# A two-block sequence model on one core: the opening and FFN edits together with another form of retention's read-out

## What is computed

```
first_block:   n = rms_norm(x); proj = n @ w_in
               ya = s5_branch(proj[:512])          # two-way state-space scan, 32 groups, GLU
               yb = sgu_branch(...)                # spatial gating
               h += (gate_a*(ya @ w_proj_a) + gate_b*(yb @ w_proj_b)) @ w_out
               h += memory_cross_attention(...)
               h += (silu(hn @ w_gate) * (hn @ w_up)) @ w_down
second_block, twice (l = 0, 1):
               z = rmsnorm(x) @ w_in[l]            # queries, keys, values of four mixers, gates
               yA = forgetting_attention   yB = dsa_attention
               r  = retention(rope(qC), rope(kC)/8, vC)       # 8 heads of 64
               yC = head_groupnorm(r) * silu(gC)   yD = sliding_window_gqa
               x += sum_n(sigmoid(gate_n) * (y_n @ w_branch_n)) @ w_out[l]
               x += (silu(a) * b) @ w_down[l]      # a, b = causal_dwconv(h @ w_up)
out = rmsnorm(x)

retention, as the kernel takes it, for head h and token n:
    r[n] = sum_{m <= n} (q[n] . k[m]) * g_h^(n-m) * v[m]
```

## Time and profile before

| | us |
|---|---|
| median of three executions | 3000.81 (3000.4 to 3000.95) |
| the profiled execution, its own time | 3000.99 |
| span of its trace | 2999.2 |
| PE busy | 2965.2 (99%) |
| DVE, ACT, POOL busy | 1559.7, 1345.9, 1308.2 |
| mean granted TensorE clock | 0.998 |

### The profile page before, as it was taken

One profiled execution on the slowest core, in us unless ns is written; L12 is line 12 of the kernel. 1 busy time (PEld: TensorE's weight loads), 2 busy tenths in 40 slices (PEclk: granted clock), 3 DMA queues, 4 the chain that ended last, 5 costly groups with the idle time before them and its releaser, 6 DMA issues.

```text
span 2999.2 us, 41533 instructions
## 1 busy us (share of the span) xinstructions
PE 2965.2 (99%) x15950; PEld 2461.9 (82%) x15950; DVE 1559.7 (52%) x2363; ACT 1345.9 (45%) x2274; POOL 1308.2 (44%) x930
## 2 busy tenths in 40 slices
PE   8999999999999999999999999999999999999998
PEld 7778887789988878888888888888788888888887
DVE  7875351497824978672116433177877521273312
ACT  5443344455533446564234443244565532354432
POOL 5335574410154543134454554554332354554443
PEclk9999999999999999999999999999999999999999
DMA  5234333233233522123333333244231233333322
GB/s 160 81 114 141 95 124 99 74 113 109 82 101 84 149 73 86 50 71 99 96 98 95 95 98 97 84 114 137 72 88 45 72 95 99 95 95 95 99 98 71
DMA packets 215043, 288.25 MB, mean 96 GB/s; under 512 B 42698, under 2 KB 122626, under 8 KB 213186
## 3 DMA queue, kind: packets, MB, share of 16 engines
q1 hardware_dynamic: 212354, 280.41, 31.4%
q0 software_dynamic: 880, 2.99, 0.3%
q10 hardware_dynamic: 1616, 2.23, 0.2%
HBM read 270.33 MB, written 4.72 MB: 92 GB/s over the span
## 4 chain that ended last, share of the span: by engine, by line
PE 92%; DVE 4%; ACT 2%; POOL 1%; issue 1%; DMA 0%; ACTq 0%; SPq 0%; DVEq 0%
PE half L871 75%; PE half L1201 2%; PE half L1204 2%; PE half L1203 2%; PE half L1354 2%; PE half L1340 2%; POOL wL L3402 1%; PE half L1411 1%; PE half L1318 1%; PE half L1323 1%; DVE arena L2388 1%; PE half L1126 0%; PE half L1143 0%; DVE rms L2379 0%; PE half L1397 0%
## 5 line engine op out<-in xcount | busy, mean ns | idle before, releaser
L3402 POOL TENSOR_TENSOR wL<-slot,wH 128x512 fp32r<-128x512 f32 (+1 forms) x904 | 1276.5, 1420 | 1661.5 <-ACT wH L1521 1660.5
L1521 ACT ACTIVATE wH<-slot 128x512 fp32r<-128x512 f32 (+1 forms) x904 | 558.2, 624 | 1074.3 <-PE half L871 1068.5
L871 PE MATMUL half<-nH,wH 128*128 128x512 f32 x2048 | 809.3, 395 | 4.5 <-ACT arena L1534 2.3
L871 PE MATMUL half<-nH,wL 128*128 128x512 f32 x2048 | 798.1, 390 | 0.0
L871 PE MATMUL half<-nL,wH 128*128 128x512 f32 x2048 | 797.7, 389 | 0.0
L871 PE MATMUL half<-arena_split,wH 128*128 128x512 f32 (+1 forms) x2432 | 736.0, 385 | 1.0 <-POOL wL L3402 0.6
L871 PEld LDWEIGHTS half<-arena_split,wH 128*128 128x128 f32 x2432 | 451.1, 188 | 94.0 <-POOL wL L3402 2.8
L871 PE MATMUL half<-arena_split,wL 128*128 128x512 f32 (+1 forms) x1216 | 466.4, 384 | 0.0
L871 PEld LDWEIGHTS half<-nH,wH 128*128 128x128 f32 x2048 | 384.4, 188 | 99.7 <-issue 19.3
L871 PEld LDWEIGHTS half<-nH,wL 128*128 128x128 f32 x2048 | 384.5, 188 | 81.9
L871 PEld LDWEIGHTS half<-nL,wH 128*128 128x128 f32 x2048 | 384.7, 188 | 78.2 <-issue 1.4
(11 more groups left out here) (404 smaller groups left out, 3656.2 us busy)
## 6 DMA issues: line engine op xcount, KB each, us to landing
slot<-in_w_in SPq DMA_DIRECT2D x344, 256.0 KB, 2.7
slot<-in_w_up SPq DMA_DIRECT2D x400, 128.0 KB, 2.2
slot<-in_w_down SPq DMA_DIRECT2D x132, 256.0 KB, 2.7
slot<-in_w_branch SPq DMA_DIRECT2D x64, 256.0 KB, 2.7
slot<-in_w_out SPq DMA_DIRECT2D x48, 256.0 KB, 2.8
arena<-arena SPq DMA_DIRECT2D x40, 256.0 KB, 4.4
slot<-in_w_gate SPq DMA_DIRECT2D x48, 128.0 KB, 2.3
arena<-in_w_gate SPq DMA_DIRECT2D x40, 128.0 KB, 2.3
```

The lines of the kernel that those rows point to most:

```text
L871: mm = pe.matmul(dst, lhsT, rhs, start=(k == 0 and m == 0), stop=(k == last and m == 2))
L1521: act.activation(wH[:, p, 0:cols], slot[:, s, 0:cols], ACT.Copy).then_inc(weights_high, 1)
L3402: pool.tensor_tensor(wL[:, p, 0:cols], slot[:, s, 0:cols], plainly(wH[:, p, 0:cols]), ALU.subtract)\
```

## The change

It has three parts. **Opening:** `plain` of the second half goes behind unit 3 of `zv0` instead of unit 1, `turn_u` and `turn_v` one or two units later, `taps(0)` one. ACT rounds the first units of `zv0` in other places, one of them ahead of its first big copy. The copies into `bd` go from POOL to ACT. SP stores `x_kept` four loads later. DVE makes `gather_taps(0)` amid `inputs_matrix(1)`. **FFN:** ACT keeps "U2" at g = 2 before it waits for S4; DVE multiplies the first two groups out earlier, one in front of P7's rest and one in front of P3's, and makes the rests of P4 and of the next P1 and P5 earlier. **Retention:** values are stationary (128 rows by 64 columns, the two heads on the two halves of the array's columns) and probabilities move (512, 384, 256 and 128 columns), which leaves channels on partitions; ACT copies that into `kC`, PE transposes it (`ret_back`), ACT copies again into `otm`. SiLU of gC goes behind the last copy.

```
-S5_STEPS = [("plain", 1, 1), ("turn_u", 0, 2), ("turn_v", 0, 3), ("taps", 0, 6), ("drive", 0, 8), ("turn_v", 1, 10),
+S5_STEPS = [("plain", 1, 3), ("turn_u", 0, 4), ("turn_v", 0, 5), ("taps", 0, 7), ("drive", 0, 8), ("turn_v", 1, 10),
...
+RETAINED = [("out", 0), ("back", 0), ("out", 1), ("back", 1), ("out", 2), ("out", 3), ("back", 2), ("back", 3)]
...
-                if n == 6:
+                if n == 10:
                     read_out(sp, "ahx0")
...
+                def retained_read(what, i):
+                    pe.wait_ge(S["heads_out_read"], PRIMED + l * ALL_OUTS + OUTS["ret"] + RETAINED.index((what, i)) + 1)
...
-                    else:
-                        pe.wait_ge(S["heads_out_read"], PRIMED + l * ALL_OUTS + OUTS["ret"] + max(i - 1, 1))
+                    elif i >= 2:
+                        retained_read("back", i - 2)
+                    for j in range(NB):
+                        for p in range(2):
+                            mm = pe.matmul(ps[i % 2][HD * p:HD * p + HD, O_AT + j * P:O_AT + T],
+                                           vC[:, j, (2 * i + p) * HD:(2 * i + p) * HD + HD],
+                                           ret_probs[:, i % 2, p, ret_at[j]:ret_at[j] + T - j * P],
+                                           start=(j == 0), stop=(j == NB - 1), skip_group_check=True)
+                    mm.then_inc(S["ret_out"], 1)
+
+                def ret_back(i):
+                    retained_read("out", i)
                     for b in range(NB):
...
+                        mm = pe.transpose(ps[i % 2][:, O_AT + b * P:O_AT + b * P + P], ret_turned[:, i, b * P:b * P + P], ident)
                     mm.then_inc(S["ret_out"], 1)
...
-                for i in range(1, PAIRS):
-                    ret_scores(i)
-                    ret_out(i - 1)
-                ret_out(PAIRS - 1)
+                ret_scores(1)
+                ret_out(0)
+                ret_scores(2)
+                ret_back(0)
+                ret_out(1)
+                ret_scores(3)
+                ret_back(1)
+                ret_out(2)
+                ret_out(3)
+                ret_back(2)
+                ret_back(3)
...
+            round_units("azv0", 0, 0, [0], 512)
             plain_x(0)
-            round_units("azv0", 0, 0, [0], 512)
+            round_units("azv0", 0, 0, [1], 512)
...
                     token_sum_high("ass_ff", 3)
+                    keep(name, "U2", "P6")
                 summed_until(act, "a", g, "S4")
                 product_high(name, "P3")
-                keep(name, "U2", "P6")
+                if g > FIRST_PRODUCTS:
+                    keep(name, "U2", "P6")
...
-            inputs_matrix(1)
-            gather_taps(0)
+            inputs_matrix(1, lambda: gather_taps(0))
```

More of the change, by code:

```diff
@@ L211 @@
 TURNS = turns_before(len(STEPS))
[L212 to L213 removed]
+OUTS = {"fox": 0, "dsa": PAIRS, "ret": 2 * PAIRS, "swa": 4 * PAIRS}
+ALL_OUTS = 5 * PAIRS
+RETAINED = [("out", 0), ("back", 0), ("out", 1), ("back", 1), ("out", 2), ("out", 3), ("back", 2), ("back", 3)]
 class Weave:
@@ L1435, in _ @@
                 pe.wait_ge(S["roped"], PRIMED + l * 6 + 6)
-                pe.wait_ge(S["heads_out_read"], PRIMED + l * ALL_OUTS + OUTS["ret"] + 3)
+                retained_read("back", 2)
                 for it in WEAVE_S.its:
@@ L1678, in _ @@
             angles_whole(0)
+            round_units("azv0", 0, 0, [2], 512)
             circle(0)
-            round_units("azv0", 0, 0, range(1, SPLITS), 512)
+            round_units("azv0", 0, 0, [3], 512)
             act.wait_ge(S["s5_bbar"], 4)
@@ L1714, in _ @@
                     plain_x(q)
+                    act.wait_ge(S["s5_zeros_set"], 2)
+                    for n in range(2):
+                        for g in range(2):
+                            at = slice(STATE * g, STATE * g + STATE)
+                            act.activation(bd[at, n, :, CHAN * g:CHAN * g + CHAN], b_bar[n][at, :, :], ACT.Copy)\
+                               .then_inc(S["s5_zeros_set"], 1)
                 elif task == "turn_u":
@@ L2228, in _ @@
                         decays(1)
[L2230 to L2233, removed]
+                for what, i in RETAINED:
+                    act.wait_ge(S["ret_out"], l * len(RETAINED) + RETAINED.index((what, i)) + 1)
+                    act.activation((ret_turned if what == "out" else otm)[:, i, :], ps[i % 2][:, O_AT:O_AT + T], ACT.Copy)\
+                       .then_inc(S["heads_out_read"], 1)
+                    if what == "out" and i + 2 < PAIRS:
                         decays(i + 2)
-                    if i == 0:
+                    if (what, i) == ("out", 0):
                         stack_high("key", "swa")
+                    if (what, i) == ("back", 0):
                         stack_high("swa", 0)
-                    if i == 1:
-                        read_out(act, "bgC", l)
-                        act.activation(gC, gC, ACT.Silu).then_inc(S["gc_ready"], 1)
+                read_out(act, "bgC", l)
+                act.activation(gC, gC, ACT.Silu).then_inc(S["gc_ready"], 1)
                 gates_used = []
@@ L2596, in split_rows, with inputs_matrix @@
                 return v.rearrange("p e (s c) -> p e s c", s=count)
-            def inputs_matrix(q):
+            def inputs_matrix(q, amid=None):
                 if q:
@@ L2607, in inputs_matrix @@
                 first = mark(dve.tensor_tensor(t[0], l_im, b_im, ALU.mult))
+                if amid:
+                    amid()
                 dve.tensor_tensor(v[1], l_re, b_im, ALU.mult)
@@ L3012, in _ @@
                     dve.sem_inc(drained[h], 1)
+                product_rest(name, "P3")
+                if g == FIRST_PRODUCTS:
+                    token_sum_rest("ass_ff", 3)
+                    product_rest(name, "P4")
+                    product_rest(following, "P1")
                 if g + 1 < NG:
@@ L3241, in weigh_retained @@
                     if i >= 2:
-                        dve.wait_ge(S["ret_out"], l * PAIRS + i - 1)
+                        dve.wait_ge(S["ret_out"], l * len(RETAINED) + RETAINED.index(("out", i - 2)) + 1)
                     for m, bank in enumerate(forward):
@@ L3421, in _ @@
             rests("axa", units=range(2, KD))
-            rests("azv0", units=range(3))
-            pool.wait_ge(weights_split, KD + 3)
-            pool.wait_ge(S["s5_bbar"], 4)
-            for n in range(2):
-                for g in range(2):
-                    at = slice(STATE * g, STATE * g + STATE)
-                    pool.tensor_copy(bd[at, n, :, CHAN * g:CHAN * g + CHAN], b_bar[n][at, :, :]).then_inc(S["s5_zeros_set"], 1)
-            pool.wait_ge(S["s5_zeros_set"], 6)
-            rests("azv0", units=range(3, KD))
-            for name in ("azv1", "azu0", "azu1", "aga0", "agb0", "aglu"):
+            for name in ("azv0", "azv1", "azu0", "azu1", "aga0", "agb0", "aglu"):
                 rests(name)
```

26 lines of the change are left out of this document (11 added, 15 removed).

## The result

The changed kernel takes 2980.82 us (median of 4 runs, 2980.21 to 2981.64) where the kernel before takes 3000.88: a ratio of 0.9934, 95% interval 0.9922 to 0.9946, 20.1 us less. The forecast was 2981.6. The profiled execution took 2980.91 with a span of 2979.1, against 3000.99 and 2999.2, so the two traces differ by the same 20.1.

The account below looks back on a forecast made before the run. PE was taken as the bound, busy for 99% of the span, so time could come only from fewer or shorter PE slots or its waits. 3000.99 - 11.8 - 2.7 - 4.7 = 2981.8 us, 2981.6 for the median; range 2978 to 2989.

Parts of the forecast that it names:

- Retention, -11.8 forecast: Retention: read-outs of 2.35 us for 4.61 and four transposes of 0.5 save 5.9 us a layer, twice.
- The two waits, 0.3 and 0.4 a layer: Retention: out3 waits 0.3 us behind DVE's weighing of pair 3, back3 waits 0.4 for the copy of out3.
- The upper bound of 4.7: Retention: a read-out takes 4.7 us, not 2.35, if the halves of the columns take turns.
- FFN, -2.7 forecast: FFN at g = 2: P7 starts 2.0 us earlier, the clock gives 1.7 more, a new wait costs some 1.0.
- the new wait: FFN: PE waits some 1.0 us before P6 of the next group, since DVE's wait for ACT's SiLU lies bare.
- 2.0 earlier, 1.7 more for the clock: FFN at g = 2: the earlier keep of U2 starts P7 2.0 us earlier; without the wait the clock stays at 2.4 GHz, 1.7 more.
- Opening, -4.7 forecast: Opening: scan(0) gains its 4.05 us wait for drive(0), plus 0.65 net from less DVE work before it.
- PE's 5.5: Opening: PE can reach drive(0) 5.5 us earlier, from 1.0 + 2.9 + 1.6.
- The term for DVE's own work getting shorter: Opening: a net gain of 0.65 us from changes to DVE's work before scan(0).
- the opening's gain is lost on DVE: Opening rival: POOL collisions or the wait in gather_taps(0) fill the 4.05 us, scan(0) starts as before; 2984 to 2987; chance 0.15.
- The copies show: Retention rival: transpositions wait for copies or weighing sets the pace, four or so waits a layer of 0.7 us; 2987; chance 0.12.
- Halves take turns: Retention rival: column halves take turns at long operands, +5.2 us instead of -11.8; 2998.6, no change; chance 0.04.

Follow-up runs that it names:

- heads in turn: The changed kernel, but a retention read-out issues one head's four matmuls and then the other's; 2991.47 us.
- That keep alone: The kernel before, with one edit: ACT keeps U2 ahead of its rounding for P3, DVE's order as before; 3003.19 us.
- late keep: The changed kernel, but ACT keeps U2 behind its rounding for P3 again, with DVE in the new order; 2982.04 us.
- the opening alone: The kernel before with only the edits of the opening; 2996.48 us.
- retention alone: The kernel before with only the edits of retention; 2988.57 us.
- the run with POOL's copies: The changed kernel, but the four copies into the block matrix stand on POOL again, between its rests for zv0 units 2 and 3; 2984.18 us.
- all four kernels with the old opening: The kernel before (3000.88 us), and it with only the retention edits (2988.57), only the FFN edits (2998.43) or only the early keep of U2 (3003.19).
- the run with the late gathering: The changed kernel, but DVE gathers the taps of quarter 0 behind inputs_matrix(1) again, not amid it; 2985.34 us.

## Why the prediction was right

**Retention, -11.8 forecast, -12.3 measured.** Right in mechanism and nearly in size. The halves of the columns run together: 2.30 a read-out, 2.35 taken; transposes 0.59, 0.5 taken. The two waits, 0.3 and 0.4 a layer, were there, 0.27 each: the last record of read-out 2 and the first of read-out 3 start 0.38 us apart (1251.617 and 1252.000), and so do the last transpose of pair 2 and the first of pair 3 (1254.690 and 1255.072), where records of 128 columns otherwise follow at 0.11. The first of them ends when DVE's weighing of pair 3 does, as foreseen. The copies are covered (0.77 each where they are not), SiLU is hidden and would cost 0.5 a layer elsewhere. The upper bound of 4.7 for heads in turn was too high: with heads in turn in the program it is 3.5 to 3.9. A change of tiling mode costs at most 0.09 us, not 0.13: at such a change the next record starts 0.20 behind one of 128 columns (1241.111 to 1241.313), not 0.11, and 0.31 behind one of 256 (1243.367 to 1243.673), not 0.22. That is also what the four transposes took over 0.5. The rule of the Trainium skill weighed there (TensorEngine Tiling (Array Packing), Key Properties), that a change of tiling mode drains the engine, shows no more than this price here.

**FFN, -2.7 forecast, -2.7 measured, for a reason told only in part.** P7 is directly behind P2, the clock stays at 1.00, and the new wait is 0.8 before P6 of the next group, for SiLU, at the place and nearly of the size foreseen. For all the edits of this part together the account holds: DVE's rest for P6 was to be done at 654.0 where it had been 655.2, and it was done at 649.55, which is 653.9 in the time of the kernel before, with the 4.3 us already gained in the opening. What failed is that it puts "2.0 earlier, 1.7 more for the clock" down to the moved keep. That keep alone puts PE 2.4 later, for DVE's rest of P4 is then the bound, a wait that the sum does not name. DVE's new order carries the stage; with it, the keep adds 1.3 (late keep against early). The number for the whole came out because the bound on DVE was right; the prediction did not weigh the earlier bound, P4's rest, which DVE's new order also took out of the way, and that much is luck. The reason given for the clock, that it stays up because the wait goes, also fell: with the opening alone and with the late keep the wait of 2.0 was there and the clock stayed.

**Opening, -4.7 forecast, -4.3 to -4.5 measured.** The choice to read the gain at scan(0), not at PE's 5.5, was right: scan(0) came 4.35 earlier, taps(1) 4.26. The term for DVE's own work getting shorter was mis-sized: 0.65 taken, 0.3 found. And the cost that the prediction feared of the gathering amid inputs_matrix(1) was its gain: there drive(0) can start, and without it 4.5 us are lost. DVE's gathering ended at 79.2 before, so PE's earlier arrival alone would have met a wait. The edits of this part don't have a price each that adds up: by shifts the copies on ScalarE are worth 2.3 and the gathering 4.9, where the whole gives 4.5. The prediction's own bounds had two slips that change little: PE's part adds up to 1.0 + 2.9 + 1.5 = 5.4, not 5.5 (5.6 measured), and the FFN without its new wait to -3.7, not -3.9. The later store of `x_kept`, costed at nothing, shows none: PE's list has no wait for a DMA but the one at its start.

On the collisions of DVE with POOL: in the changed kernel one of DVE's operations of the same shape takes 2.44 us beside a rest of 1.29 (both start at 59.9) and 1.34 to 1.35 without, the 1.1 of the earlier trace rows again. The exclusive lock on the port pair of the Trainium skill (SBUF — State Buffer) agrees with it.

**The rivals.** Of "the opening's gain is lost on DVE" the place was right and the price small: the waits at out(0) and taps(1), 0.7 each. "The copies show" needs another order than the one made. "Halves take turns" needs another order of the loops. No short wait in retention drew the clock down, not even four of 0.77 a layer.

## What to carry to other kernels

Before a wait is priced at its length, look at what the other engines do meanwhile: undoing the longest wait of a stage alone put PE 2.4 us later in the trace (1.7 by the medians, within their interval), because a second engine had used that wait to catch up. When products have 64 output rows for each of two heads, issue the heads' matmuls alternately on the two halves of the columns, with the long operand moving; the same eight matmuls took 2.30 us alternating and 3.86 in turn. The copy that a transposition needs costs nothing when a read-out or scores of 2.3 us stands between, and 0.77 us when nothing does.

## What the hardware showed beyond what was expected

- **Matmuls pass one another.** With heads in turn, a matmul on one half of the columns started 0.21, 0.43 and 0.54 us before three that stand ahead of it in the program on the other half. The Trainium skill (TensorE: Matmul & The Clock Gate, Part 3) says that matmuls start strictly in the order of the program; in this trace the starts of records don't, and the measurement decides.
- **The same wait, with and without a fall of the clock.** A wait of 2.0 us before P7 was followed by half the clock in the kernel before (0.51) and with retention alone (0.50), and not with the opening alone, nor with the late keep (both 1.00). Nor was the 2.6 us of the run with POOL's copies. Around the wait of 2.9 us before line 946 or 947 it fell in all four kernels with the old opening, from 0.4 us before the wait's end to 1.4 us behind it, and in the waits of 3.5 and 4.0 us it was at half already when PE went on. Behind the 2.0 us it fell 1.2 and 1.4 us after PE had gone on. So near 2 us the length of a wait alone does not say whether the clock falls. What else decides was not tried and stays open. The prediction says that in its trace a fall followed only the two waits of 2 us and more; PE also stands 2.9 and 5.6 us in the first 9 us. The views give 1.00 there, but the transposes start 0.21 us apart until 13.6 and 0.11 apart behind it, the spacing at half and at full clock, so in that stretch 1.00 is not to be trusted.
- **A late half costs twice.** In the run with the late gathering, the wait of 4.0 us was followed by drive(0) at 1.2 GHz, 3.68 us where it takes 2.08 at 2.4 GHz, and DVE stood 3.90 us until that was done.
